# Feed-forward loop chunks with the weights as stationary operand, in products of 256 columns

## What is computed

```python
def rms_norm(x, g):
    xf = x.astype(jnp.float32)
    y = xf * lax.rsqrt(jnp.mean(xf * xf, axis=-1, keepdims=True) + EPS)
    return (y * g.astype(jnp.float32)).astype(x.dtype)

def swiglu(x, w_in, w_out):
    gate, up = jnp.split(x @ w_in, 2, axis=-1)
    return (jax.nn.silu(gate) * up) @ w_out

# in first_block, twice per layer, two layers:
h = swiglu(rms_norm(x, g[0]), w_ffn_in[layer, 0], w_ffn_out[layer, 0])
x = x + 0.5 * rms_norm(h, g[1])
```

## Time and profile before

| | |
|---|---|
| median of 3 runs | 1382.19 us (1381.94 to 1382.32) |
| profiled execution, its own time | 1381.7 us |
| its span, first to last instruction | 1379.8 us (1.9 us lie around it) |
| PE busy | 1358.3 us, 98% |
| POOL busy | 1134.6 us, 82% |
| ACT busy | 660.2 us, 48% |
| DVE busy | 462.9 us, 34% |

### The profile page before, as it was taken

One profiled execution on the slowest core, in us unless ns is written; L12 is line 12 of the kernel. 1 busy time (PEld: TensorE's weight loads), 2 busy tenths in 40 slices (PEclk: granted clock), 3 DMA queues, 4 the chain that ended last, 5 costly groups with the idle time before them and its releaser, 6 DMA issues.

```text
span 1379.8 us, 18197 instructions
## 1 busy us (share of the span) xinstructions
PE 1358.3 (98%) x6396; PEld 1115.6 (81%) x6396; DVE 462.9 (34%) x1134; ACT 660.2 (48%) x741; POOL 1134.6 (82%) x912
## 2 busy tenths in 40 slices
PE   6999999999999999999999999999999999999997
PEld 5888888888888888888888778888888888888886
DVE  6100134654000156310001885000146125762224
ACT  5444445546444455544444676444446444544531
POOL 5999987849999977999998539999977987679882
PEclk9999999999999999999999999999999999999999
DMA  7666554537656545666655426655545554346550
GB/s 256 213 205 205 185 198 151 183 104 226 193 190 193 190 168 180 203 195 199 194 184 183 138 71 210 202 193 192 183 153 198 183 183 152 124 153 235 184 175 31
DMA packets 160958, 246.95 MB, mean 179 GB/s; under 512 B 8924, under 2 KB 99844, under 8 KB 160772
## 3 DMA queue, kind: packets, MB, share of 16 engines
q1 hardware_dynamic: 158612, 239.42, 53.2%
q10 hardware_dynamic: 2288, 6.75, 1.3%
HBM read 245.10 MB, written 1.05 MB: 178 GB/s over the span
## 4 chain that ended last, share of the span: by engine, by line
POOL 59%; PE 22%; issue 17%; DMA 1%; ACT 1%; DVE 0%; POOLq 0%; ACTq 0%; SPq 0%; DVEq 0%
POOL w_lo L553 59%; PE acc L1858 5%; PE acc L1861 5%; PE acc L1859 5%; PE gu L1858 1%; PE gu L1861 1%; PE gu L1859 1%; PE tb L1861 1%; PE tb L1859 1%; PE tb L1858 1%; PE tb L2394 1%; PE gu L2359 0%; PE tb L2368 0%; DMA x_res<-in_x 0%; DMA w_raw<-in_w_in 0%
## 5 line engine op out<-in xcount | busy, mean ns | idle before, releaser
L553 POOL TENSOR_TENSOR w_lo<-w_raw,w_hi 128x512 fp32r<-128x512 f32 x896 | 1129.5, 1304 | 218.3 <-ACT w_hi L582 218.1
L582 ACT CAST w_hi<-w_raw 128x2048 fp32r<-128x2048 f32 x225 | 425.1, 1909 | 122.0 <-DMA w_raw<-in_w_ffn_in 33.6
L1858 PE MATMUL gu<-w_hi,xT_hi 128*128 128x512 f32 x832 | 330.4, 397 | 3.8 <-DVE w_lo L1782 2.8
L1859 PE MATMUL gu<-w_lo,xT_hi 128*128 128x512 f32 x832 | 324.2, 390 | 0.0
L1861 PE MATMUL gu<-w_hi,xT_lo 128*128 128x512 f32 x708 | 276.5, 391 | 0.0
L1858 PE MATMUL acc<-w_hi,xT_hi 128*128 128x512 f32 x496 | 198.2, 400 | 0.0
L1859 PE MATMUL acc<-w_lo,xT_hi 128*128 128x512 f32 x496 | 193.2, 389 | 0.0
L1858 PEld LDWEIGHTS gu<-w_hi,xT_hi 128*128 128x128 f32 x832 | 156.7, 188 | 35.6 <-DVE xT_lo L1184 3.2
L1861 PE MATMUL acc<-w_hi,xT_lo 128*128 128x512 f32 x468 | 182.7, 390 | 0.0
L1859 PEld LDWEIGHTS gu<-w_lo,xT_hi 128*128 128x128 f32 x832 | 156.9, 189 | 31.1 <-issue 0.2
L1861 PEld LDWEIGHTS gu<-w_hi,xT_lo 128*128 128x128 f32 x708 | 133.1, 188 | 28.5
(11 more groups left out here) (329 smaller groups left out, 1360.4 us busy)
## 6 DMA issues: line engine op xcount, KB each, us to landing
w_raw<-in_w_ffn_in SPq DMA_DIRECT2D x176, 512.0 KB, 4.6
w_raw<-in_w_ffn_out SPq DMA_DIRECT2D x88, 512.0 KB, 4.1
w_raw<-in_w_in SPq DMA_DIRECT2D x80, 512.0 KB, 4.4
w_raw<-in_mlstm_w_in SPq DMA_DIRECT2D x24, 512.0 KB, 4.6
w_raw<-in_w_ple_gate SPq DMA_DIRECT2D x16, 512.0 KB, 4.1
w_raw<-in_w_kv SPq DMA_DIRECT2D x16, 512.0 KB, 4.6
w_raw<-in_mlstm_w_out SPq DMA_DIRECT2D x8, 512.0 KB, 4.1
w_raw<-in_diff_w_q SPq DMA_DIRECT2D x8, 512.0 KB, 4.2
```

The source lines that it names most:

```text
L553: ins = pool.tensor_tensor(w_lo[:, slot.spl, cols], w_raw[:, slot.raw, cols], w_hi[:, slot.spl, cols].bitcast(F32), ALU.subtract)
L582: nc.scalar.copy(w_hi[:, slot.spl, :], w_raw[:, slot.raw, :]).then_inc(hi_ready, 1)
L1858: mm(out, xh, wh, start=(half == 0 and k == 0), stop=False)
L1859: mm(out, xh, wl, start=False, stop=False)
```

## The change

In the loop chunks the roles are exchanged. The stationary operand is now a 128 x 128 block of weights, the moving one 256 columns of x transposed, all tokens at once. The result stands with hidden columns on partitions and tokens along the columns, so that nothing has to be transposed ahead of the next product. A chunk's 256 gate and 256 up columns make four groups of rows; each group is accumulated in one half of a bank of its own (`gu[:, 0]`, `tb[:, 1]` for gate, `gu[:, 1]`, `tb[:, 0]` for up). Since the norm factor now runs along columns, it is spread once per stage into a row form `rs_row` (two transposes of `rstd`, copied by DVE), and DVE multiplies each of the four groups by it in place. Silu comes then without a scale, in two instructions; DVE multiplies it in; ACT rounds and DVE subtracts, each in two halves. Results of even chunks go to new buffers `hE_hi`, `hE_lo`, of odd chunks to `hT_hi`, `hT_lo`.

```diff
+                def gate_up_rows(n, i, a):
+                    for half in range(2):
+                        slot = a.plus(half)
+                        pe.wait_ge(lo_ready, slot.count())
+                        for r, rows in enumerate((gate_rows(0), gate_rows(1), up_rows(0), up_rows(1))):
+                            if half == 0 and r == 0:
+                                pe.wait_ge(h_ready, i * 4 + (2 * NIT * f + 2 * n))
+                            if half == 0 and r == 2:
+                                pe.wait_ge(ht_lo_ready, i * 2 + ht_count(f, n - 1))
+                            for k in range(4):
+                                w = slice(512 * k + P * r, 512 * k + P * r + P)
+                                out, at = rows[:, 0:2 * P], 4 * half + k
+                                mm(out, w_hi[:, slot.spl, w], xT_hi[:, at, :], start=(half == 0 and k == 0), stop=False)
+                                mm(out, w_hi[:, slot.spl, w], xT_lo[:, at, :], start=False, stop=False)
+                                last = mm(out, w_lo[:, slot.spl, w], xT_hi[:, at, :], start=False,
+                                          stop=(half == 1 and k == 3))
+                            if r >= 2:
+                                last.then_inc((tile0_used, slot_used)[r - 2], 1)
+                            elif half == 1:
+                                last.then_inc(gate_in_psum, 1)
...
+                def turn_rstd():
+                    c = 2 * PRE[name]
+                    pe.wait_ge(rstd_ready, c + 2)
+                    for t in range(TILES):
+                        ins = nc.tensor.transpose(tb[:, 1, tok(t)], rstd[:, c + t:c + t + 1].broadcast_to([P, P]),
+                                                  ident[:])
+                    ins.then_inc(rs_row_in_psum, 1)
...
+                turn_rstd()
                 down_n(0, None, At(s0 + 4))
-                turn_h(1, None, hs_next if name in SKEWED else hs)
+                turn_h(1, hs_next if name in SKEWED else hs)
+                pe.wait_ge(rs_row_ready, f + 1)
                 with pe.Fori(0, (NIT - 3) // 2) as i:
                     for d in (0, 1):
-                        gate_up(2 + d, i, At(s0 + 5 + 3 * d, i))
+                        gate_up_rows(2 + d, i, At(s0 + 5 + 3 * d, i))
                         down_n(1 + d, i, At(s0 + 7 + 3 * d, i))
-                        turn_h(2 + d, i)
```

ACT's part of a loop chunk:

```diff
+                def by_rows(n, i, a):
+                    ahead(a)
+                    ahead(a.plus(1))
+                    for j in range(2):
+                        act.wait_ge(gate_scaled, i * 4 + row_count(f, n, 2, j))
+                        act.wait_ge(h_ready, i * 4 + (2 * NIT * f + 2 * (n - 1) + j + 1))
+                        nc.scalar.activation(sg[:, j, :], gate_rows(j)[:, 0:2 * P], ACT.Silu).then_inc(silu_ready, 1)
+                    ahead(a.plus(2))
+                    for j in range(2):
+                        act.wait_ge(h_ready, i * 4 + (2 * NIT * f + 2 * n + j + 1))
+                        nc.scalar.copy(h_rows(n)[0][:, j, :], up_rows(j)[:, 0:2 * P]).then_inc(row_hi_ready, 1)
```

DVE's part:

```diff
+                def take_row():
+                    dve.wait_ge(rs_row_in_psum, f + 1)
+                    v.tensor_copy(rs_row, tb[:, 1, 0:2 * P]).then_inc(rs_row_ready, 1)
+
+                def by_rows(n, i):
+                    def scaled(rows):
+                        return v.tensor_tensor(rows[:, 0:2 * P], rows[:, 0:2 * P], rs_row, ALU.mult)
+
+                    for j in range(2):
+                        dve.wait_ge(gate_in_psum, i * 4 + row_count(f, n, 2, j))
+                        scaled(gate_rows(j)).then_inc(gate_scaled, 1)
+                    for j in range(2):
+                        dve.wait_ge((tile0_used, slot_used)[j], At(s0 + 3 * n, i).count())
+                        scaled(up_rows(j)).then_inc(row_step, 1)
+                        dve.wait_ge(row_step, i * 4 + row_count(f, n, 2, j))
+                        dve.wait_ge(silu_ready, i * 4 + (2 * NIT * f + 2 * n + j + 1))
+                        u = up_rows(j)[:, 0:2 * P]
+                        v.tensor_tensor(u, u, sg[:, j, :], ALU.mult).then_inc(h_ready, 1)
+                    hi, lo = h_rows(n)
+                    for j in range(2):
+                        dve.wait_ge(row_hi_ready, i * 4 + row_count(f, n, 2, j))
+                        ins = v.tensor_tensor(lo[:, j, :], up_rows(j)[:, 0:2 * P], hi[:, j, :].bitcast(F32), ALU.subtract)
+                    ins.then_inc(ht_lo_ready, 1)
```

More of the change, by code:

```diff
@@ L284, in program @@
         ht_lo_ready = sem("ht_lo_ready")
+        rs_row_in_psum = sem("rs_row_in_psum")
+        rs_row_ready = sem("rs_row_ready")
+        gate_in_psum = sem("gate_in_psum")
+        row_step = sem("row_step")
+        gate_scaled = sem("gate_scaled")
+        row_hi_ready = sem("row_hi_ready")
         consts_ready = sem("consts_ready")
@@ L342, in ht_count, with turned_count, row_count, gate_rows @@
             return (NIT + 1) * f + n + 1 + t
+        def turned_count(f, n, t=0):
+            return 4 * f + (3 + t if n == NIT - 1 else min(n, 1) + 1)
+        def row_count(f, n, per, i):
+            return per * ((NIT - 3) * f + n - 2) + i + 1
+        def gate_rows(j):
+            return (gu[:, 0, :], tb[:, 1, :])[j]
+        def up_rows(j):
+            return (gu[:, 1, :], tb[:, 0, :])[j]
+        def h_rows(n):
+            return (hT_hi, hT_lo) if n % 2 else (hE_hi, hE_lo)
         wg_split = sem("wg_split")
@@ L668, in silu @@
                         if n:
-                            act.wait_ge(h_ready, turns(4, 2 * NIT * f + 2 * (n - 1) + t + 1))
+                            act.wait_ge(h_ready, 2 * NIT * f + 2 * (n - 1) + t + 1)
                         else:
@@ L1927, in ffn @@
                 f, s0 = FFN_NO[name], S[name]
-                def gate_up(n, turn, a):
-                    if n:
-                        pe.wait_ge(h_ready, 2 * NIT * f + 2 * n if turn is None else turn * 4 + 2 * NIT * f + 2 * n)
-                    across(a, 0, [gu[:, t, :] for t in range(TILES)])
-                    across(a.plus(1), 1, [gu[:, t, :] for t in range(TILES)])
+                def gate_up_rows(n, i, a):
[18 more added lines that the diff above has]
+                                last.then_inc(gate_in_psum, 1)
@@ L1936, in down_n @@
                 def down_n(n, turn, slot):
                     pe.wait_ge(ht_lo_ready, ht_count(f, n) if turn is None else turn * 2 + ht_count(f, n))
+                    hi, lo = h_rows(n) if n else (hT_hi, hT_lo)
                     for t in range(TILES):
-                        down_tile(slot, hT_hi, hT_lo, t, n == 0, False)
-                def turn_h(n, turn, source=hs):
+                        down_tile(slot, hi, lo, t, n == 0, False)
+                def turn_rstd():
[5 more added lines that the diff above has]
+                    ins.then_inc(rs_row_in_psum, 1)
@@ L1944, in turn_h @@
+                def turn_h(n, source=hs):
                     if n == 0 and name in SKEWED:
@@ L1982, in ffn @@
                     across_tile(At(s0 + 2), 0, 1, gu[:, 1, :])
-                    turn_h(0, None)
+                    turn_h(0)
                     across_tile(At(s0 + 3), 1, 1, gu[:, 1, :])
```

54 lines of the change are left out of this document (29 added, 25 removed).

## The result

The changed kernel took 1390.88 us (median of 5 runs, 1389.36 to 1391.13), the kernel before, on the same chip, 1382.32 (1381.94 to 1383.02). The ratio is 1.0057, with an interval of 1.0046 to 1.0067: slower by 0.6%, where the likeliest case of the prediction was no difference that counts. Its profiled execution has an own time of 1390.88 us and a span of 1388.9, that is 9.1 more than the 1379.8 before.

What follows compares the result with a forecast made beforehand. PE, 98% busy at 2.4 GHz, was taken as the bound. From 1381.7 us, -3.5 (loops) + 1.0 (row form) + 0.3 (F0) = -2.2 gave 1379.5; the runs' median being 0.5 higher, 1380.0, range 1376 to 1396.

Steps and rivals of the forecast that it cites:

- the price of a 256-column product: In the loops' gate and up rows: 0.117 us per product, 96 per chunk, 0.34 us more per chunk.
- The one row that paired them: Earlier trace: a 128-column load beside a 256-column product, next start as far off as behind an 8-column load.
- Rival (a): Weight load bounds the loop products: 111 + 10 = 121 ns each, 1392 us; decides from 118.6 ns; chance 20%.
- Rival (b): Weight loads in the loops do not overlap products at all: 218 ns a product, 1690 us; chance 2%.
- Rival (c): PE's sequencer gives one load and product pair only each 0.124 us in the loops: 1402 us; chance 5%.
- Rival (d): Faster: the loop products' distance is 0.111 us, 18 us less in all, 1362 us; chance 8%.
- Rival (e): DVE and ACT exchange outlasts its cover, PE waits once a chunk: 1412 us with 1 us each; chance 5%.
- (f): The change does not do what it says; excluded for the transposes, since 32 of 40 go.
- The transposes: Four transposes and the restart behind them leave each loop chunk on PE: 0.46 us less per chunk.
- The down products: `down_n` keeps its 24 products per chunk, 5.44 us, plus 0.01 us for the change from short to long products.
- The row form: Two transposes per stage ahead of `down_n(0)`, 0.25 us each time: 1.0 us more over four stages, on PE.
- F0's thin place: F0's chunk 3: the third group wants the low part at 64.8, ready at 65.0; 0.3 us more, once.

Runs made afterwards that it cites:

- half loads: The changed kernel with 64 instead of 128 weight columns in every loop product, the stream left at 256 columns: 1371.06 us.
- 240 columns: The changed kernel with only the first 240 of the 256 columns streamed in every loop product, weight load unchanged: 1366.09 us.
- the run with one transpose: The kernel before, with one transpose instead of four for each loop chunk, all waits, copies and products kept: 1371.8 us.
- the kernel with sixteen of a kind: The changed kernel with w_hi products joined to 512 columns, ordered per chunk as 16 long, 16 short, 16 short, 16 long: 1378.14 us, ratio 0.9964.
- the kernel with two banks: The changed kernel with the two groups of a pair alternating product by product, so no bank gets two in a row: 1389.41 us, ratio 1.0054.
- one long and one short in turn: The changed kernel with w_hi products joined to 512 columns, alternating with 256-column w_lo products, 64 products a chunk: 1381.27 us, ratio 0.9993.
- groups of four: The changed kernel with joined 512-column w_hi products, four long then four short, reversed in the second slot: 1379.37 us, ratio 0.9982.
- the sweep: The changed kernel with stream lengths from 192 to 256 columns and 8 to 128 weight columns, set per group by a table: 1373.36 us.

## Why the prediction was wrong, and where it was right

**The step that failed is the price of a 256-column product.** I had it as the longer of two things, each from a row in which the other was short: 117 ns from products with 8 weight columns, and loads of 111 ns. Together they take 120.0. The term 96 x 0.117 - 10.89 = +0.34 us measured 96 x 0.120 - 10.89 = +0.63, and over 32 chunks that is 9.2 of the 10.9 us by which 1380.0 was missed. The one row that paired them, 228.43 to 228.55 in the earlier trace rows, stood at the head of a new row; in the changed kernel, too, the first distance behind long products is 113 and the second 119. That one event said nothing of the settled distance. I had put this down as "one event and not a long row", and still gave it the weight of the main reason. The reason that I gave for the +0.34 failed too, "since a short product pays its fixed part twice": with half loads the 96 short products take the same 10.89 us as the 48 long ones, so the whole +0.63 belongs to the full load beside a stream of its own length.

**Rival (a) had the size by luck, and not the mechanism.** It named 121 ns and 1392 us, against 120.0 and 1390.9. But it added a fixed 10 ns to the load, and with 240 columns the load stands at 111.7 with nothing added. What the runs show in its place is a surcharge of up to 6.8 ns where load and stream are about equally long. The 120.0 lies beyond the 118.6 ns from which I had said that the case decides.

**Rival (b),** that loads do not overlap, fell by far: 120 ns and not 218. In its section "The mechanism" (the prediction named the section behind it) the page "TensorE: Matmul & The Clock Gate" of the Trainium skill has this rule, overlap only with another row group. The trace does not agree: all products here are of one row group, and pairs with a full load take 111.7 ns. The page's own section "Step-by-step: what each phase is for" lets a load run ahead into a second weight buffer, and with that the traces agree.

**Rival (c),** supply, fell: with 240 columns and 64 weight columns the pairs go out every 106.8 ns, and in the changed kernel at 120. The 62 ns that stand behind its 124 are given in the Trainium skill ("TensorE: Matmul & The Clock Gate", "Wait — 56ns, not 53.3ns?") for a product, and only with hardware decode off; no run here shows which way of decoding the chip used. **Rival (d)** came true only for other sizes: with 240 columns the distance is the load's. **Rival (e)** fell: in the changed kernel PE waits for DVE in no loop chunk, and with 16 passes of DVE instead of 8 in none either but for F0's chunk 3 (below). **(f)**, as I had said, did not arise.

**The transposes** were worth what I had put, 0.46 us a chunk: three of the four were 0.33 in the run with one transpose, and 17.41 - 16.98 = 0.43 is what the turning makes between two kernels with the same 96 products. **The down products** after the short ones cost more than I had allowed, 5.47 instead of 5.44 plus 0.01, 0.6 us in all. **The row form** cost 0.9 us against 1.0. **F0's thin place** cost nothing against 0.3: in chunk 3 the 96 products take 11.51 us as in any other chunk. It was no invention, though; in the kernel with sixteen of a kind the third group comes already 8 x 0.226 = 1.8 us into the chunk's products and not 24 x 0.120 = 2.9, and its waits have a single one for `hE_lo` (the kernel with 240 columns has one too, 0.6 us):

```profile
PE gu L2017 <- DVE hE_lo L1312: 1.0, 1, 1.0
```

**The seam between F1 and F2,** 1.7 us, I had not seen, and the change has nothing in it that touches this place. ACT's and PE's timelines of the changed kernel there (in brackets the idle time before, and who ended it):

```profile
547.33 0.34 ACTq L616 DMA_DIRECT2D arena<-in_norm_g  x1
547.70 2.10 ACTq L1137 DMA_DIRECT2D arena<-in_p  x1
```

```profile
562.96 0.50 PE L1922 MATMUL gu<-w_hi,xT_hi 128*128 128x512 f32 x1 [0.81 <-POOL w_lo L579]
567.92 0.50 PE L1922 MATMUL gu<-w_hi,xT_hi 128*128 128x512 f32 x1 [0.62 <-POOL w_lo L579]
```

Issuing the load of `in_p` held ACT's queue for 2.10 us, where it took 0.47 before. The slot that ACT rounds next is late by as much, POOL's passes behind it too, and PE waits twice. In the kernel with two banks the same line looks like this, and PE has no wait for POOL at all (its span is 1386.8):

```profile
547.25 0.46 ACTq L1137 DMA_DIRECT2D arena<-in_p  x1
```

So this is a part that comes and goes: the issue took 1.6 us in the profiled runs of the kernels with one long and one short in turn and with groups of four, and 0.46 or 0.47 in those of the eleven others, the kernel before among them. It may account for part of the spread of the changed kernel's runs, 1389.4 to 1391.1. The DMA records of the traces hold a hint: in all three slow cases a transfer of instructions of 16 KB is under way during the issue (in the changed kernel from 0.37 us before its start to 1.71 behind it, and the issue ends at 2.10), and in the eleven others none is. That is a coincidence in three of three; no run tested it as the cause.

**The sum again,** with measured terms, against the span: +6.2 (loops, forecast -3.5), +0.9 (row form, 1.0), -0.3 (where F0's loop begins; 0.3 more had been forecast for its chunk 3), and, not of the change, +1.7 (seam) and +0.7 (the first 17 us) = 9.2, where 9.1 were found. Without the last two the changed kernel would still be some 7 us slower; the profiled run with two banks, which has no seam and 0.2 instead of 0.7 in the first 17 us, has a span 7.0 us above the kernel before.

What stays open is the cause of the surcharge. Shown is that it changes with the lengths of stream and load, those of the neighbours in the row included; that it stays the same with the roles of the operands exchanged, with two banks in turn, and with blocks that repeat; and that the sequencer can supply pairs faster than every 120 ns.

## What to carry to other kernels

A product's price must be read from a long row of the very pair, the stream's length and the load's length together; the larger of two prices from rows in which one of them was small is too low just where they are close. Here halving the stream to 256 columns brought it level with the load, and that cost 20 us (32 x 0.63), more than the 15 us that the transposes gave. Where two products share their stationary operand, join their streams, and keep long and short products in long rows of their own kind: that turned 1390.9 us into 1378.1 with the same columns streamed, and some more work for DVE.

## What the runs showed of the hardware

- Stream and load of nearly the same length, beside each other, take longer than either: 113.2 and 111.7 ns give 120.0. At 272 columns a full load costs 3.0 ns more than half a one, at 320 and above nothing that is clear of the 0.5 ns (or more, next to another length) to which a group of twelve can be read.
- What a stream of this type costs above its columns at 2.4 GHz is neither a fixed amount nor a fixed share: 6.8 ns at 240 columns (106.8 instead of 100) and 6.5 at 256 (both with 64 weight columns), about 13 at 320, 384 and 512 (226.7 instead of 213.3), and 20 at 448 (206.7 instead of 186.7, measured with full loads only). In the earlier trace rows I had read a fixed 10 ns, and built rival (a) on it.
- With 256 columns and loads of only 8 the distance is 115.6 ns in the sweep and 117 in the earlier trace rows, more than the 113.2 with loads of 32 or 64; with 512 columns loads of 64, 32 and 8 take 230 to 232 ns, against 226.6 with 128. A smaller load is not always the cheaper one.
- A change from short products to long ones costs up to 14 ns on the first long one (241 instead of 226.7, one long and one short in turn). In a long row it wears off: behind the 32 short ones in the kernel with sixteen of a kind the long ones take 233, 236, 228, 233 and 230 ns, then 227.
